# Variance of the four folded norms: squares added by GpSimd, one matrix product behind the fourth query product

## What is computed

```python
def layer_norm(x, g, b):
    xf = x.astype(F32)
    mu = jnp.mean(xf, -1, keepdims=True)
    var = jnp.mean(jnp.square(xf - mu), -1, keepdims=True)
    return ((xf - mu) * lax.rsqrt(var + LN_EPS) * g.astype(F32) + b.astype(F32)).astype(x.dtype)

def post_norm(x, h, g, b):
    return layer_norm(ALPHA * x + h.astype(x.dtype), g, b)
...
        yp = post_norm(yp, hp, ln_g[l, 0], ln_b[l, 0])
...
        yp = post_norm(yp, cross_attn(yp, mk, mv, mem_wq[l], mem_wo[l]), ln_g[l, 1], ln_b[l, 1])
...
        yp = post_norm(yp, peer_ffn(yp, peer_wq[l], peer_subkeys[l], peer_u[l], peer_v[l]), ln_g[l, 2], ln_b[l, 2])
```

## Time and profile before

| | us |
|---|---|
| median of 3 runs | 2272.33 |
| lowest, highest | 2271.83, 2275.17 |
| span of the profiled execution | 2273.0 |
| TensorE busy | 2195.2 (97%) |
| VectorE busy | 1679.6 (74%) |
| ScalarE busy | 1316.6 (58%) |
| GpSimd busy | 1018.2 (45%) |

### The profile page before, as it was taken

One profiled execution on the slowest core, in us unless ns is written; L12 is line 12 of the kernel. 1 busy time (PEld: TensorE's weight loads), 2 busy tenths in 40 slices (PEclk: granted clock), 3 DMA queues, 4 the chain that ended last, 5 costly groups with the idle time before them and its releaser, 6 DMA issues. The chain is left out here.

```text
span 2273.0 us, 45901 instructions
## 1 busy us (share of the span) xinstructions
PE 2195.2 (97%) x15489; PEld 1975.8 (87%) x15489; DVE 1679.6 (74%) x3923; ACT 1316.6 (58%) x3010; POOL 1018.2 (45%) x819
## 2 busy tenths in 40 slices
PE   8989899999999999999989898999999999999998
PEld 8878699999999877888879877999999997788887
DVE  7866489969999756666646555899599996566666
ACT  6545365557776545555556444645677765555555
POOL 6764347997777500000043243489877774000000
PEclk9999999999999999999999899999999999999999
DMA  7548454554444655555544583455544446555554
GB/s 256 159 147 325 165 178 147 172 175 156 156 158 149 222 195 185 185 186 187 190 140 142 184 352 112 150 167 168 175 155 154 157 149 232 190 189 185 185 187 136
DMA packets 112423, 409.33 MB, mean 180 GB/s; under 512 B 16553, under 2 KB 18769, under 8 KB 107089
## 3 DMA queue, kind: packets, MB, share of 16 engines
q1 hardware_dynamic: 107744, 391.45, 51.3%
q0 software_dynamic: 4528, 15.86, 2.2%
HBM read 397.11 MB, written 10.14 MB: 179 GB/s over the span
## 5 line engine op out<-in xcount | busy, mean ns | idle before, releaser
L2045 POOL TENSOR_TENSOR slab_ring_lo<-slab_ring,u_hi 128x512 fp32r<-128x512 f32 x512 | 678.0, 1347 | 174.4 <-ACT u_hi L2141 173.6
L2087 PE MATMUL banks<-operand_hi,u_hi 128*128 128x264 f32 x2048 | 594.3, 290 | 1.8 <-POOL slab_ring_lo L2045 1.8
L2089 PE MATMUL banks<-operand_hi,slab_ring_lo 128*128 128x264 f32 x2048 | 583.4, 285 | 0.0
L2088 PE MATMUL banks<-operand_lo,u_hi 128*128 128x264 f32 x2048 | 582.7, 285 | 0.0
L270 POOL TENSOR_TENSOR slab_ring_lo<-slab_ring,slab_hi 128x512 fp32r<-128x512 f32 x161 | 218.8, 1364 | 630.6 <-ACT slab_hi L260 629.8
L2529 DVE TENSOR_TENSOR operand_lo<-slab_ring,operand_hi 128x512 fp32r<-128x512 f32 x508 | 350.2, 691 | 134.3 <-ACT operand_hi L2491 114.7
L2584 PE MATMUL banks<-operand_hi,w_hi 128*128 128x512 f32 x1000 | 398.3, 398 | 4.8 <-DVE w_lo L2525 4.8
L2585 PE MATMUL banks<-operand_hi,w_lo 128*128 128x512 f32 x1000 | 396.4, 396 | 0.0
L2586 PE MATMUL banks<-operand_lo,w_hi 128*128 128x512 f32 x1000 | 396.3, 396 | 0.0
L2141 ACT ACTIVATE u_hi<-slab_ring 128x512 fp32r<-128x512 f32 x512 | 322.1, 631 | 120.5 <-PE banks L2089 120.0
L2087 PEld LDWEIGHTS banks<-operand_hi,u_hi 128*128 128x128 f32 x2048 | 386.8, 189 | 4.0 <-POOL slab_ring_lo L2045 3.1
(11 more groups left out here) (427 smaller groups left out, 3773.0 us busy)
## 6 DMA issues: line engine op xcount, KB each, us to landing
slab_ring<-in_u SPq DMA_DIRECT2D x256, 512.0 KB
slab_ring<-in_v SPq DMA_DIRECT2D x256, 512.0 KB
slab_ring<-in_proj SPq DMA_DIRECT2D x144, 512.0 KB
cache_k_T<-in_cache_k SPq DMA_DIRECT2D x16, 1024.0 KB, 9.2
cache_v<-in_cache_v SPq DMA_DIRECT2D x16, 1024.0 KB, 12.8
memory_T<-in_mem POOLq DMA_DIRECT2D x2, 1024.0 KB, 6.6
sample_state<-in_state POOLq DMA_DIRECT2D x8, 256.0 KB, 4.2
out_mem_k_out<-mem_k_T SPq DMA_DIRECT2D x16, 128.0 KB, 2.2
```

Source lines behind the costliest of these rows:

```text
L2045: nc.gpsimd.tensor_tensor(step.ring_lo[:, s, g * HC:(g + 1) * HC, :], step.slab(s)[:, g * HC:(g + 1) * HC, :], hi[:, buf].bitcast(F32), AL ...
L2087: nc.tensor.matmul(bank, hi[:, buf, k, :], xh[:, c, :], start=(c == 0), stop=False)
L2088: nc.tensor.matmul(bank, hi[:, buf, k, :], xl[:, c, :], start=False, stop=False)
L2089: last = nc.tensor.matmul(bank, step.ring_lo[:, s, c, :], xh[:, c, :], start=False, stop=(c == DC - 1))
```

## The change

In each of the four blocks GpSimd adds the squares in place once all eight are there: chunks 4 to 7 to chunks 0 to 3 (1056 columns in one instruction), then 2 to 2 (528), then 1 to 1 (264). These stand behind its halves of query slabs 2, 3 and 4. TensorE makes one product with the sum, behind query product 3, where before it made eight behind query product 1. ScalarE takes the square root behind slabs 4 and 5 and columns 2 and 3, and VectorE does its halves of slabs 4 and 5 ahead of the reciprocal.

```diff
+SUMS_FROM, VAR_BEHIND = 2, 3
...
-            if k == 1:
-                for j in range(DC):
-                    pe.wait_ge(self.squared, j + 1)
-                    last = nc.tensor.matmul(var, step.mean_d, self.squares[:, j, :], start=(j == 0), stop=(j == DC - 1))
-                last.then_inc(self.var, 1)
+            if k == VAR_BEHIND:
+                pe.wait_ge(self.summed, 3)
+                nc.tensor.matmul(var, step.mean_d, self.squares[:, 0, :], start=True, stop=True).then_inc(self.var, 1)
...
         columns(1)
-        act.wait_ge(self.var, 1)
-        nc.scalar.activation(step.rstd[:], step.ps[:, VAR_BANK, 0:T], ACT.Sqrt, bias=step.eps).then_inc(self.std, 1)
         for n in range(4, 6):
             split_high(step, act, self.query + n)
             columns(n - 2)
+        act.wait_ge(self.var, 1)
+        nc.scalar.activation(step.rstd[:], step.ps[:, VAR_BANK, 0:T], ACT.Sqrt, bias=step.eps).then_inc(self.std, 1)
...
-        split_low(step, dve, self.query + 2, (1,))
-        split_low(step, dve, self.query + 3, (1,))
+        for n in range(2, QUERY_BANKS):
+            split_low(step, dve, self.query + n, (1,))
         dve.wait_ge(self.std, 1)
...
-        split_low(step, dve, self.query + 4, (1,))
...
         correct(0)
-        split_low(step, dve, self.query + 5, (1,))
         correct(1)
...
+            level = j - DC - SUMS_FROM
+            if 0 <= level < 3:
+                half = DC >> (level + 1)
+                pool.wait_ge(self.squared, DC)
+                if level:
+                    pool.wait_ge(self.summed, level)
+                nc.gpsimd.tensor_tensor(self.squares[:, 0:half], self.squares[:, 0:half], self.squares[:, half:2 * half],
+                                        ALU.add).then_inc(self.summed, 1)
```

## The result

Six executions of the changed kernel have a median of 2280.88 us (2275.99 to 2287.08), six of the kernel before on the same chip 2272.08 us. The ratio is 1.0041, 95% interval 1.0025 to 1.0056: 5.7 to 12.7 us slower. A second set on another occasion gave 2277.47 against 2271.45 us, ratio 1.0031 (1.0019 to 1.0043). The forecast was 2275.7 us, its range ended at 2279.5.

The account below looks back on a forecast made before the run. Beside TensorE, VectorE was taken to bound the ends of the cross blocks and the DMA queue the mixer blocks. Terms 1.85 + 1.55 + 0 + 0 = +3.4 us on 2272.3 gave 2275.7 us, range 2270.3 to 2279.5.

Parts of the forecast that it names:

- Product 3 ends at 304.9.: TensorE in cross_0: product 3 starts at 301.95 after waiting for slab 3's half, takes 2.97 us, ends at 304.9.
- Product 4 ahead by 1.05 us.: TensorE in cross_0: product 4 begins at 305.65 instead of 306.70, all that is left of 2.94 us removed.
- First addition: GpSimd in cross_0: adding 1056 columns takes 2.25 us, at most 2.62, from 298.35 to 300.6.
- Slab 3's half: GpSimd in cross_0, behind the first addition: runs 300.6 to 301.9 instead of 298.96 to 300.23.
- second addition: GpSimd in cross_0, behind slab 3's half: adding 528 columns takes 1.06 us, ending at 303.0.
- Reciprocal 6.1 us later, +1.85 us: VectorE in cross_0: reciprocal at 307.6, later by 6.1 us; waits absorb part, slab 9 and block end 1.85 us later.
- The table load as a term of 1.28 on the path: ScalarE in cross_0: square root's table load, 1.28 us, no longer hidden beside variance products, delays the reciprocal behind product 3.
- Cross_1 at +1.55, for the 0.29 us wait of the earlier trace: End of cross_1: longer by 1.55 us, since VectorE waits 0.29 us before its last correction.
- Mixers at 0: mixer_0 and mixer_1: no change, bounds -2 to +0.5 us each, since slab transfers join a full DMA queue.
- The gain stays whole: Rival, all four blocks: waits cost nothing, TensorE's 2.94 us come off each, 11.8 us, 2260 to 2266; chance 0.05.
- TensorE keeps its lead: Rival, cross blocks: they end by TensorE, 1.05 us earlier each, -2.1 in all, 2270 us; chance 0.18.
- The loop slips further: Rival, VectorE from reciprocal to slab 9, cross blocks: +1.5 us more each, 2278.7; decides from reciprocal past 308.2; chance 0.27.

Follow-up runs that it names:

- the filler: The changed kernel with five unused fp32 products on TensorE behind query product 2, where it paused; ratio to the kernel before 1.0019.
- e5: The changed kernel with ScalarE's square-root table load moved ahead of slabs 4 and 5, behind the second set of columns; ratio to the kernel before 1.0051.
- e9: The changed kernel with five unused fp32 products behind query product 2 and the table load ahead of slabs 4 and 5; ratio to the kernel before 1.0009.

## Why the prediction was wrong

- **"Product 3 ends at 304.9."** This step failed. TensorE's pause was foreseen (1.75 us, 2.23 measured), but product 3 was priced at the 2.97 us of the earlier trace rows with nothing for the clock. It took 4.58, and 3.2 at full clock. That brings 1.3 us at the end of each cross block when the clock falls, as it did 6 times of 8: the forecast's +3.4 us become about +6, and the cross blocks of the first trace hold +6.6. The size of this step is shown by two traces of one kernel and by the filler. It doesn't cover the whole miss: with it the forecast is 2278.3 to 2278.9, inside the range, whose end the median passed by 1.4 us (the second set's, 2277.47, did not). The last 2 us lie outside the cross blocks and stay open, as below.
- **"Product 4 ahead by 1.05 us."** Wrong as well. Counted from the first centred chunk product 4 begins at 11.55 us at full clock and 12.34 in the first trace, 11.64 before: 0.1 ahead, or 0.7 behind. Of the 2.94 us taken from TensorE nothing was left there.
- **The other terms.** First addition 2.46 (2.25 said, 2.62 the bound). Slab 3's half 1.71 (1.27 said) and second addition 1.75 (1.06 said, nothing kept above it): too low by 0.4 and 0.7, since VectorE's shares of slabs 3 and 4 stand beside them, 3.62 us for two. The Trainium skill, page "SBUF — State Buffer", section "SBUF: two separate sides", lets whichever of the two started first hold the pair for its whole instruction; the forecast applied this to VectorE's loop and not to GpSimd's own queue ahead of it, where the trace agrees with it as well (1.71 and 1.75 against 1.27 and 1.06).
- **Reciprocal 6.1 us later, +1.85 us.** At full clock 6.9 later and +2.0: mechanism and size were right, with two errors that cancel (the reciprocal 0.8 later than reckoned; from it to slab 9's share 14.0 us, a wait of 0.42 among them, for 14.55). In the first trace it was 8.4 later and +3.3. The place of VectorE's waits was right: one of 0.42 is left of 2.9.
- **The table load as a term of 1.28 on the path.** Right for the reciprocal in the first trace, which came 1.24 us earlier without it (e5), wrong for the end at full clock: hidden, it gave nothing there (e9).
- **Cross_1 at +1.55, for the 0.29 us wait of the earlier trace rows.** Wrong: that wait was one execution's. The second trace of before has 49.11 there, and the excess is the same 2.0 as in cross_0.
- **Mixers at 0.** Right as far as can be told: 1.0001 for them alone, interval 0.9991 to 1.0012. Mixer_1 under the full change is less sure, as its 27.9 and 28.1 us show.
- **The rivals.** "The gain stays whole" and "TensorE keeps its lead" fell. "The loop slips further" came, past its point of decision (reciprocal later than 308.2; it was 309.25 + 0.61 = 309.9 on before's clock), but by the clock, which its text doesn't name. At full clock the reciprocal was at 308.35, and the cross blocks came to +4.0 us, just short of 4.5.
- **Open.** The two sets of the changed kernel differ, +8.8 and +6.0 us, and their cross blocks hold 4.0 to 6.6 us; mixer_1 and unchanged code hold the rest. Within the first set the execution at a mean clock of 0.990 spans 2274.1 us and the one at 0.985 spans 2285.0: much of the rest goes with falls of the clock in unchanged code. Whether the change brings them about or they come by chance, the runs don't tell.

## What to carry to other kernels

Before work is taken from TensorE, ask what that work was hiding for the next product: here, of 2.9 us removed, 2.2 became a pause, and behind the pause the next product could run at half the clock. Before moving a scalar chain such as variance to reciprocal behind later work, find out how late its follower may be: here 5.1 us cost nothing, and nearly all beyond went into the end. Making one link of the chain shorter (the table load) gave nothing at full clock, where another engine's work held the next operation. A small share of the work on the helper engine, in a stretch where it stands idle (one addition of 528 columns for two products), beat the full share.

## What the chip did that was not expected

- A TensorE pause of 2.23 us, the same to 0.02 us in eight passes, was followed by 1.2 GHz in six of them and not in two; pauses of 1.5 us never were. Product 3 then takes 4.58 us instead of 3.2. What tells the six from the two was not tested. The Trainium skill, page "TensorE: Matmul & The Clock Gate", section "What's actually happening", says that the monitor behind the gate runs free of the kernel's start, so that one kernel meets it differently from run to run. It tells this of the first matmuls of a kernel; the two traces of the changed kernel show the like for a pause inside one, 0.50 behind it in one trace and 1.00 in the other.
- Five useless products in a pause made a kernel faster: 1.0009 with them (e9) against 1.0051 without (e5), intervals apart. For the change itself it is 1.0019 against 1.0031 and 1.0041, intervals that overlap, with the cross blocks' 1.3 us beside them.
- GpSimd's operations stretch as VectorE's do: a half of 1.27 us took 1.71, 1.75 and 1.81 beside VectorE's shares, an addition of 264 columns 1.20 instead of 0.75 (e5, mixer_1). And VectorE's operation behind the reciprocal took 0.30 us alone and 0.52, 0.97, 1.04 and 1.34 where GpSimd's half of a slab ran beside it.
